# Reordering the refill of a Strassen-type product's right operand, the merges behind it, and two weight loads ahead of it

## The reference, cut to what matters

```
gates   = sigmoid(h @ w_ga), sigmoid(h @ w_gb)
merged  = gate_a * (y_a @ w_pa) + gate_b * (y_b @ w_pb)
out     = merged @ w_out
```

## Time and profile before

| | |
|---|---|
| time, median of 3 runs | 1777.67 us (1777.54 to 1778.43) |
| the profiled execution: time, span | 1778.43 us, 1776.8 us |
| mean granted TensorE clock | 0.997 |
| PE, DVE, ACT busy | 98%, 65%, 37% of the span |
| stages of this stretch | gates 693 to 845 us, branch projections 845 to 1003 us |

### The profile page before, as it was taken

The page is one execution under the profiler, slowest core; times in us unless marked ns, Lnnn a source line. Parts: engine busy times, 40 slices in busy tenths (PEclk is TensorE's granted clock), DMA queues, the critical chain, the costliest instruction groups (busy, mean ns, idle before and its releaser), DMA issues.

```text
span 1776.8 us, 23266 instructions
## 1 busy us (share of the span) xinstructions
PE 1732.9 (98%) x8523; PEld 1456.0 (82%) x8523; DVE 1153.8 (65%) x1741; ACT 651.6 (37%) x1019; POOL 186.6 (11%) x244
## 2 busy tenths in 40 slices
PE   6899999999999999999999999999999999999997
PEld 3698988989888888888787888888888888888886
DVE  4677636565456767766788746856556556566657
ACT  6534241423233324445554414534333334211112
POOL 1002020200212000111122200000000001222210
PEclk9999999999999999999999999999999999999999
DMA  8211110212069123787685723122222322722212
GB/s 311 71 41 44 60 48 24 84 34 72 12 208 311 40 83 116 251 290 252 239 282 180 249 88 119 58 80 71 94 71 74 115 71 73 294 95 94 96 46 95
DMA packets 112136, 219.29 MB, mean 123 GB/s; under 512 B 6802, under 2 KB 75554, under 8 KB 106946
## 3 DMA queue, kind: packets, MB, share of 16 engines
q1 hardware_dynamic: 95394, 161.57, 26.6%
q0 software_dynamic: 16672, 56.77, 9.2%
HBM read 168.98 MB, written 49.33 MB: 123 GB/s over the span
## 4 chain that ended last, share of the span: by engine, by line
PE 89%; DVE 7%; ACT 2%; issue 2%; DMA 1%; DVEq 0%; SPq 0%; ACTq 0%
PE PD L2251 14%; PE PM L2678 11%; PE PD L2678 11%; PE PM L2552 7%; PE PD L2698 7%; PE PD L2552 7%; PE PM L2698 6%; PE PD L2583 4%; PE PD L2361 4%; PE PD L2267 4%; PE PM L2434 2%; PE PM L2613 1%; PE PD L2374 1%; PE PD L2613 1%; PE PM L2527 1%
## 5 line engine op out<-in xcount | busy, mean ns | idle before, releaser
L2251 PE MATMUL PD<-R_hi,whi 128*128 128x512 f32 x352 | 110.1, 394 | 0.0
L966 POOL TENSOR_TENSOR w_raw<-w_raw,g2B 128x2048 f32<-128x2048 f32 x11 | 50.9, 4623 | 558.8 <-DMA w_raw<-in_w_ff 394.8
L2251 PE MATMUL PD<-R_lo,whi 128*128 128x512 f32 x352 | 108.6, 390 | 0.0
L2251 PE MATMUL PD<-R_hi,wlo 128*128 128x512 f32 x352 | 108.5, 389 | 0.0
L2037 DVE TENSOR_TENSOR ws_lo<-S,ws_hi 128x512 fp32r<-128x512 f32 x76 | 56.4, 743 | 76.4 <-ACT ws_hi L1367 76.4
L2251 PEld LDWEIGHTS PD<-R_hi,wlo 128*128 128x128 f32 x352 | 66.1, 188 | 14.0
L2251 PEld LDWEIGHTS PD<-R_lo,whi 128*128 128x128 f32 x352 | 66.1, 188 | 14.0
L2251 PEld LDWEIGHTS PD<-R_hi,whi 128*128 128x128 f32 x352 | 65.2, 188 | 13.0 <-issue 0.2
L2267 PE MATMUL PD<-whi,R_hi 128*128 128x256 f32 x256 | 72.7, 284 | 0.8 <-ACT vaug L1059 0.8
L2267 PE MATMUL PD<-wlo,R_hi 128*128 128x256 f32 x256 | 72.4, 283 | 0.0
L2267 PE MATMUL PD<-whi,R_lo 128*128 128x256 f32 x256 | 72.4, 283 | 0.0
(11 more groups left out here) (494 smaller groups left out, 5028.7 us busy)
## 6 DMA issues: line engine op xcount, KB each, us to landing
rawF<-in_w_ff SPq DMA_DIRECT2D x44, 512.0 KB, 5.0
ada<-in_w_ada POOLq DMA_DIRECT2D x32, 512.0 KB, 6.0
raw<-in_w_in SPq DMA_DIRECT2D x30, 512.0 KB, 4.8
g_dram<-snapG POOLq DMA_DIRECT2D x48, 256.0 KB, 5.2
f_dram<-Fo SPq DMA_DIRECT2D x11, 1024.0 KB, 4.8
w_raw<-in_w_ff SPq DMA_DIRECT2D x11, 1024.0 KB, 5.0
f_raw<-f_dram SPq DMA_DIRECT2D x11, 1024.0 KB, 7.0
ada_raw<-in_w_ada SPq DMA_DIRECT2D x8, 1024.0 KB, 19.0
```

Of the source, the lines that this page charges most:

```text
L966: nc.gpsimd.tensor_tensor(w2_raw[par], w2_raw[par], g2B[:, :].unsqueeze(1).to_broadcast([P, 2, D]), ALU.mult)\
L2251: i = mm(dst[:, e * HALF:e * HALF + width], wk[:, k, :], part, start=(k == 0 and step == 0), stop=(k == KT - 1 and step == 2))
```

## The change

It alters only orders and one wait:

- `FILL_ORDER` is new: the refilled quarters are counted in the order 0, 3, 1, 2, 4, 5, 6. `IN_RING` becomes (3, 6): those two quarters are loaded beforehand, not 0 and 1. ACT rounds 0, 3, 1, 2 behind products 2 to 5 of the fill's block (before: 0, 1, 2, 3 behind products 0, 1, 5, 6); DVE subtracts them behind products 3 to 6 (before: three behind 1, 2, 6 and the fourth behind product 0 of the next block). Quarters 4, 5, 6 stay where they were.
- SP: the loads of `rawG` for blocks 1 and 2 are put behind the waits for the stored `y_b` and behind the first `sums_load`. In blocks 7 and 11 the load of `rawG` for block b+3 also waits for product (b+1, 1).
- `MERGE_AT`: merges 12, 13 go from (11, 4) to (12, 4); 14, 15 from (12, 3) to (12, 5); those of blocks 12 to 15 are put in pairs, partly earlier and partly later; `MOVE_AT` becomes a rule with one move behind each of the products 3 to 6 of blocks 13 and 14.
- In block 15, parts 3 and 4 are rounded together behind product 3, and part 4 is subtracted behind product 4.

```diff
+FILL_ORDER = (0, 3, 1, 2, 4, 5, 6)
 MERGE_AT = {(9, 0): (0, 1), ...
-            (10, 1): (8,), (10, 4): (9,), (10, 5): (10,), (10, 6): (11,), (11, 4): (12, 13), (12, 3): (14, 15),
-            (13, 0): (16,), (13, 2): (17,), (13, 3): (18,), (13, 5): (19,), (13, 6): (20,),
-            (14, 1): (21,), (14, 2): (22,), (14, 3): (23,), (14, 5): (24,), (14, 6): (25,),
-            (15, 0): (26,), (15, 1): (27,), (15, 2): (28,), (15, 4): (29,), (15, 5): (30,), (15, 6): (31,)}
-MOVE_AT = {(13, 3): (0,), (13, 4): (1,), (13, 5): (2,), (13, 6): (3,), (14, 3): (0, 1), (14, 4): (2,), (14, 5): (3,)}
+            (10, 1): (8,), (10, 4): (9,), (10, 5): (10,), (10, 6): (11,), (12, 4): (12, 13), (12, 5): (14, 15),
+            (13, 0): (16, 17), (13, 2): (18, 19), (14, 0): (20, 21), (14, 2): (22, 23),
+            (15, 0): (24, 25), (15, 2): (26, 27), (15, 3): (28,), (15, 4): (29,), (15, 5): (30,), (15, 6): (31,)}
-        IN_RING = (0, 1)
+        IN_RING = (3, 6)
             gate_block(0)
-            sp.wait_ge(right_ready, 4)
-            gate_block(1)
-            sp.wait_ge(left_ready, PRODUCTS)
-            gate_block(2)
             sp.wait_ge(yb_out, 16 * KT)
             sp.wait_ge(mod_io, 32)
             sp.wait_ge(sv_done, KT + 2)
             sp.wait_ge(spill, 16 * HEADS + 1)
             sums_load(0)
+            sp.wait_ge(right_ready, 4)
+            gate_block(1)
+            sp.wait_ge(left_ready, PRODUCTS)
+            gate_block(2)
 ...
+                    sp.wait_ge(product, (b + 1) * PRODUCTS + 2)
 ...
-            HI_AFTER = {0: 0, 1: 1, 5: 2, 6: 3}
+            HI_AFTER = {2: 0, 3: 3, 4: 1, 5: 2}
-            M_HI_AFTER = {0: (0, 1), 1: (2,), 2: (3,), 3: (4,), 5: (5, 6)}
+            M_HI_AFTER = {0: (0, 1), 1: (2,), 3: (3, 4), 5: (5, 6)}
-            LO_AFTER = {1: 0, 2: 1, 6: 2}
-            LO_LATER = {0: 3, 1: 4, 2: 5, 3: 6}
-            M_LO_AFTER = {1: (0, 1), 2: (2,), 3: (3, 4), 6: (5, 6)}
+            LO_AFTER = {3: 0, 4: 3, 5: 1, 6: 2}
+            LO_LATER = {1: 4, 2: 5, 3: 6}
+            M_LO_AFTER = {1: (0, 1), 2: (2,), 3: (3,), 4: (4,), 6: (5, 6)}
 ...
-                        pe.wait_ge(branch_ready, UNITS + fill * PRODUCTS + n + 1)
+                        pe.wait_ge(branch_ready, UNITS + fill * PRODUCTS + FILL_ORDER.index(n) + 1)
```

More of the change, by code:

```diff
@@ L636, in place_load @@
                     if fill:
-                        sp.wait_ge(branch_ready, UNITS + n + 1)
+                        sp.wait_ge(branch_ready, UNITS + FILL_ORDER.index(n) + 1)
                 else:
@@ L1310, in _ @@
                         branch_hi(FILL.index(b - 1), HI_LATER[n])
-                    for i in MOVE_AT.get((b, n), ()):
-                        m_move(b - 1, i)
+                    if b in (GB - 3, GB - 2) and n >= 3:
+                        m_move(b - 1, n - 3)
                     if last:
@@ L1919, in branch_lo @@
             def branch_lo(fill, n):
-                dve.wait_ge(branch_hi_d, fill * PRODUCTS + n + 1)
+                dve.wait_ge(branch_hi_d, fill * PRODUCTS + FILL_ORDER.index(n) + 1)
                 v.tensor_tensor(gate_right_lo[n], place_f32(n), gate_right_hi[n].bitcast(F32), ALU.subtract)\
```

## The result

The changed kernel takes 1809.44 us (median of 4 runs, 1806.18 to 1811.9), the kernel before beside it 1777.61 (4 runs). The ratio is 1.0178, with a 95% interval of 1.016 to 1.0197. So it is 31.8 us slower. I had forecast 1797, with a range of 1786 to 1804: the sign was right, and the time lies 5.4 us above the range.

What follows compares the result with a forecast made beforehand. PE, busy 98% of the span, was taken as the bound, so only its waits cost time. 8.3 + 2.1 + 6.1 + 2.3 + 0.8 = 19.6 us on 1778.43, less 0.76 to the median, gave 1797, range 1786 to 1804.

Steps and rivals of the forecast that it cites:

- Block 0, pause: Before product (0, 4): PE stalls 8.3 us (5.7 to 11) for ACT's snapshot, held behind the moved rawG load.
- Low clock behind it: Behind the pause in block 0: TensorE at half speed for a time, 2.1 us lost (0 to 3).
- more than the sum: Rival: block 0 loads at the 10.0 us rate and low clock behind the fills too; 1803 to 1810, chance 12%.
- The fills: Blocks 7, 8, 11, 12: DVE's later subtractions and quarter 0's late load cost 2.3 and 3.8, together 6.1 us.
- The walk through DVE's queue: Fill 0: quarters 1, 2 and 6 late by 1.8, 0.7 and 1.5 us, at least 1.7 us more per fill.
- 0.6 more: Fill 0: quarter 0's late load holds the snapshot and left operand (8, 3) behind it, 0.6 us.
- 2.1 more: Fill 1: quarter 0's load lands at 916.6, ACT ready at about 914.5, 2.1 us.
- Merges 12 to 15: Block 13, before product 3: later gate loads and quad 15's store delay the first snapshot; stall 2.3 us (0 to 4).
- Block 15: Before the output projection: merge 28's load is issued only behind merge 26; 0.8 us later (-0.5 to +2).
- no stall in block 0: Rival: rawG lands by 703 or y_b completes much earlier, leaving the last three terms, 9.2 us; 1787, chance 8%.
- the clock stays up: Rival: no low clock and loads land quickly, 9.6 us in the extreme; 1787 to 1792, chance 17%.
- faster: Rival: both waits of each fill vanish (4.8 us) and rawG for block 1 lands in time; 1773, chance 4%.

Runs made afterwards that it cites:

- p_loads_first: Kernel before with the rawG loads for blocks 1 and 2 moved behind the stored y_b but ahead of the first sums_load; 1786.85 us, ratio 1.005.
- p_fill_ring03: Kernel before with only the new fill order, but quarters 0 and 3 loaded beforehand and quarter 6 behind its product; 1782.62 us, ratio 1.0026.
- p_merge12: Kernel before with only merges 12 to 15 moved, from (11, 4) and (12, 3) to (12, 4) and (12, 5); 1784.7 us, ratio 1.0038.
- p_loads: Kernel before with only the rawG loads for blocks 1 and 2 moved behind the stored y_b and first sums_load; 1789.53 us, ratio 1.0067.
- p_spwait: Kernel before with only SP's added wait in blocks 7 and 11, rawG for block b+3 behind product (b+1, 1); 1779.33 us, ratio 1.0007.
- p_fill: Kernel before with only the new order of the refilled quarters, 3 and 6 loaded beforehand; 1791.83 us, ratio 1.0077.
- p_fill_lofirst: Kernel before with the new fill order, and DVE subtracting quarters 4, 5, 6 ahead of left operand and sums; 1790.72 us, ratio 1.0074.
- b_lofirst: Kernel before with DVE subtracting quarters 4, 5, 6 ahead of left operand and sums in blocks 8 and 12; 1773.64 us, ratio 0.9979.
- p_loads_busy: Kernel before with the two rawG loads moved behind y_b and sums_load, plus 36 unused matmuls before (0, 4)'s wait; 1787.48 us, ratio 1.0057.

## Why the forecast was wrong, point by point

The mechanisms stood nearly as forecast; the sum of 19.6 was too small, against 31.2 in the trace. I give each term as forecast and as measured.

- **Block 0, pause: 8.3 forecast, 9.9 measured.** The wait for `y_b`, the place in ACT's queue and the resume were right. The landing was taken as 7.2 us, the middle of 4.3 and 10.0; it was 9.0. p_loads_first shows the 1 MB load ahead as the reason for part of it: 6.4 without it.
- **Low clock behind it: 2.1 forecast, 2.5 measured.** Near, and in part by luck. The size came from a row that does not show what an idle does: the clock had fallen as that idle of 2.55 us began, behind 32 small matmuls, and not in the course of it (0.96 in 56 to 58 us):

```profile
58.00:60.00 2.00, 0.00 (x0) 0.00 (x0) 1.69 (x6) 1.49 (x2) 0.00 (x0) 0.50 0.00 0
```

- **Low clock behind other pauses: not in the sum, 6.2 measured** (1.7 + 1.7 behind the fills, 2.8 in block 13). This is the step that failed most. The prediction puts the low clock in one place only and gives no reason for leaving it out at the others. It had them at 2.3 us in block 13 and at 1.8 to 2.4 in fill 0; but in fill 1 its own terms, 1.8 for DVE's queue and 2.1 for the late load, already make up to 3.9, longer than either idle of the earlier trace rows. They came out at 3.5, 4.4 and 4.0. The rival "more than the sum" held it for the fills, with 12%, and not for block 13.
- **The fills: 6.1 forecast, 9.4 measured without the low clock.** The walk through DVE's queue was right: p_fill_ring03 shows it within about 0.1 us for each wait of fill 0, and in the whole change (12, 1) and (12, 6) come out at 1.8 and 1.4. What was too small is "0.6 more" and "2.1 more" for quarter 0's load. p_fill_ring03 puts 9.2 us on it, low clock included. I had it land 7.2 us after its issue; it took 9.8 and 10.8. And I had not followed to PE what a late rounding on ACT holds. I named the snapshot behind (7, 3) as held, but priced it only by what DVE does later; PE waited for it, and for that behind (11, 3), before products (7, 5) and (11, 5), 1.6 and 4.4 us, and the signs that I gave have no idle there.
- **Merges 12 to 15: 2.3 forecast, 4.0 measured**, at the upper bound. The held snapshot ended 14.9 us after the start of (12, 6), not 13.2. I had reckoned 0.5 us from merges 12 and 13 to the issue of the gate loads; that for quad 15 took 2.1 behind the stores on POOL. p_merge12 shows the stall is this one edit.
- **Block 15: +0.8 forecast, -0.8 measured.** The wait before the output projection is 1.2 in place of 2.0. It scatters between kernels that don't touch it: 2.8 in p_loads, 1.4 in p_spwait. So neither number says much.
- **The wait of SP: 0 forecast, 1.7 us above before in the median and not told from 0**, with no wait of PE behind it in the trace. Right, as far as it can be measured.

Of the 11.6 us that were lacking, 6.2 are low clock behind pauses that had none in the sum; 3.3 more are waits in the fills, 1.7 in block 13, 1.6 in block 0, 0.4 the clock there, less 1.6 in block 15. Late landings of loads are behind the waits in the fills and in block 0. The range did not save it: even with every term at its upper bound (11 + 3 + 9 + 4 + 2 = 29) the sum gives 1807, for the low clock at the other pauses is in none of them. The late loads of block 0 and the fills all had 1 MB just ahead on the same queue and were late in the same execution; my range cut off the end where all are late, as if they were independent. That they share the cause is my reading; only block 0 was tested for it, by p_loads_first.

Of the rivals, "no stall in block 0" and "the clock stays up" are refuted by the timeline and the windows above, "faster" by the waits before (8, 1) and (12, 1). The nearest is "more than the sum" (1803 to 1810), and 1809.4 is at its far end.

Not settled: why quarter 0's load is slower in fill 1 than in fill 0. From its issue to ACT's rounding it takes 10.8 against 9.8 us here, 11.2 against 9.1 in p_fill and 10.6 against 9.8 in p_fill_lofirst; no run varied the traffic beside it alone.

## What to carry to other kernels

Before putting a wait for a DMA into an engine's queue, look at what stands behind it there: here a snapshot that TensorE needed 2 us later, and the same in both fills. Cost each pause of TensorE that may come near the ones here (3.5 us and more) with the half-speed stretch behind it (1.7 to 2.8 us), and take landing times that may share a cause as late together. Where VectorE serves both this block and the next, put what is due in this block first: that order alone gave 4.1 us in b_lofirst, which was more than the kernel before had left to win at any other single place.

## What the runs showed of the hardware that I had not expected

- On one issuing queue, two loads of 512 KB land 4.3 us after issue alone, 6.4 us in p_loads_first (four issued together), and 9.0 us with a 1 MB load just ahead. A 1 MB load behind 1 MB of weights took 9.8 and 10.8 us.
- The low clock costs as much behind a pause of 4.0 us (2.8) as behind one of 9.9 (2.5), and 1.7 us behind 3.5 and 4.4 us. Behind the same pause of 3.5 us before (8, 1) it costs 1.7, 1.5 and 2.8 us in three kernels (the changed one, p_fill, p_fill_lofirst). Behind a loss of 3.06 us before (12, 1) in p_fill_ring03 there is one of 1.6 us, behind 3.03 us at the same place in p_fill none, and in the kernel before an idle of 3.58 us near its start was followed by none. So the length of the pause alone does not set it, and no run here shows what else does.
- The clock can also fall with no pause ahead: at 134 to 136 us of the changed kernel it is 0.50 with PE busy throughout, where the same code ran at 1.00 in the profiled execution of the kernel before.
- Filling a pause of 9.9 us with 36 matmuls whose result is not used kept the clock at 1.00 (p_loads_busy).
